# Adding up the token rows during the final expert item, and finishing only that item's 128 slots after it

## What is computed

```python
def moe_swiglu(x, w_router, b_router, w_g, w_u, w_d):
    logits = (x @ w_router).astype(jnp.float32) + b_router.astype(jnp.float32)
    top_v, top_i = lax.top_k(logits, TOP_K)          # TOP_K = 2 of 8 experts
    top_w = jax.nn.softmax(top_v, axis=-1)
    ...
    for e in range(N_EXPERTS):
        y = y + combine[..., e:e + 1] * swiglu(x, w_g[e], w_u[e], w_d[e])
    return y
...
x = layer_norm(ALPHA * x + f, p['ln2_g'][l], p['ln2_b'][l])
```

## Time and profile before

| | us |
|---|---|
| median of 3 runs (1659.34 to 1661.12) | 1660.32 |
| the profiled execution: its time | 1659.13 |
| the profiled execution: its span | 1657.3 |
| last matmul of the last item ends | about 1616.3 |
| from there to the end of the span | 41.0 |

### The profile page before, as it was taken

The page is one execution under the profiler, slowest core; times in us unless marked ns, Lnnn a source line. Parts: engine busy times, 40 slices in busy tenths (PEclk is TensorE's granted clock), DMA queues, the critical chain, the costliest instruction groups (busy, mean ns, idle before and its releaser), DMA issues.

```text
span 1657.3 us, 20014 instructions
## 1 busy us (share of the span) xinstructions
PE 1584.7 (96%) x7315; PEld 1265.9 (76%) x7315; DVE 1155.0 (70%) x1312; ACT 810.4 (49%) x1093; POOL 178.0 (11%) x115
## 2 busy tenths in 40 slices
PE   8999999999999999999999999789999999999990
PEld 7877777888888888888777788467777777777770
DVE  6888747584444423379887584698888888888886
ACT  5344442253223222163444422667777777777771
POOL 0410005151000000005000060200000000000006
PEclk9999999999999999999999999899999999999995
...
DMA packets 134380, 325.69 MB, mean 197 GB/s; under 512 B 7984, under 2 KB 19632, under 8 KB 133808
## 3 DMA queue, kind: packets, MB, share of 16 engines
...
## 4 chain that ended last, share of the span: by engine, by line
PE 94%; DVE 3%; ACT 1%; DMA 1%; issue 1%; POOL 0%; SPq 0%; ACTq 0%; DVEq 0%
PE bank L1312 15%; PE bank L1313 15%; PE bank L1314 15%; PE bank L1593 9%; PE bank L1595 9%; PE bank L1594 9%; PE bank L1352 4%; PE bank L1351 4%; PE bank L1350 4%; PE bank L1601 3%; PE bank L1572 1%; PE bank L1424 1%; PE bank L1437 1%; DVE X L1182 1%; PE bank L1409 1%; PE bank L1305 1%
## 5 line engine op out<-in xcount | busy, mean ns | idle before, releaser
L821 DVE TENSOR_TENSOR wlo<-raw,whi 128x1024 fp32r<-128x1024 f32 x170 | 239.0, 1408 | 207.5 <-ACT whi L522 207.2
L1312 PE MATMUL bank<-xth,whi 128*128 128x512 f32 (+1 forms) x976 | 381.5, 391 | 1.8 <-DVE wlo L821 1.8
L1313 PE MATMUL bank<-xtl,whi 128*128 128x512 f32 (+1 forms) x976 | 370.8, 380 | 0.0
L1314 PE MATMUL bank<-xth,wlo 128*128 128x512 f32 (+1 forms) x976 | 370.5, 380 | 0.0
L1045 DVE TENSOR_TENSOR ewlo<-eraw,ewhi 128x2048 fp32r<-128x2048 f32 x135 | 309.0, 2290 | 66.8 <-ACT ewhi L717 66.7
L717 ACT ACTIVATE ewhi<-eraw 128x2048 fp32r<-128x2048 f32 x135 | 258.0, 1911 | 43.0 <-PE bank L1595 43.0
L522 ACT ACTIVATE whi<-raw 128x1024 fp32r<-128x1024 f32 x170 | 178.6, 1051 | 137.0 <-PE bank L1352 123.9
L1312 PEld LDWEIGHTS bank<-xth,whi 128*128 128x128 f32 x976 | 184.2, 189 | 50.7 <-issue 8.5
L1313 PEld LDWEIGHTS bank<-xtl,whi 128*128 128x128 f32 x976 | 184.2, 189 | 36.4 <-issue 3.8
L1593 PE MATMUL bank<-ewhi,xgh 128*128 128x512 f32 (+1 forms) x528 | 205.9, 390 | 6.0 <-DVE xgl L1112 4.8
L1314 PEld LDWEIGHTS bank<-xth,wlo 128*128 128x128 f32 x976 | 184.1, 189 | 35.3
...
## 6 DMA issues: line engine op xcount, KB each, us to landing
...
raw<-dense_w SPq DMA_DIRECT2D x170, 512.0 KB, 3.4
...
rows<-item_rows ACTq DMA_DIRECT2D x11, 512.0 KB, 7.2
```

Source lines behind the costliest of these rows:

```text
L821: V.tensor_tensor(wlo[:, g % SPL, :], raw[:, g % RAW, :], whi[:, g % SPL, :], ALU.subtract).then_inc(lo_done, 1)
L1312: mm(out, wh, xh, start=first, stop=False)
L1313: mm(out, wh, xl, start=False, stop=False)
L1314: return mm(out, wl, xh, start=False, stop=last)
```

## The change

The final item is taken out of the loop and written out behind it on every engine, without the preparations for a next item. In the routing stage DVE also works out, for each token, whether one of its two rows lies in the final item (`inl`), the weights of the rows that don't (`wrest`, 0 for one that does) and gather indices (`gidx`, row 0 for one that does); a small matmul with a 0/1 matrix `sel_last` gives for each of the final item's 128 slots its token, weight and whether it is used (`mslot`). In the first item eight tiny DVE steps (`last_slots`) turn these into indices.

During the final item POOL gathers the eight tiles of result rows of the items before through three buffers, and DVE adds them to `X` in turn (`add_rest`), one behind each `e_low` from piece step 5 on, and two behind the last. SP stores the four sums to `xd`. ACT takes the mean and variance of tiles 0 to 2 by running sums and normalises them, DVE does tile 3, and DVE applies gain and bias to tiles 0 to 2 (`affine_out`); SP stores all four. These rows are right for every token that has no row in the final item. For the final item's 128 slots POOL gathers the sums back from `xd`, DVE adds the weighted result rows straight from PSUM, normalises them and POOL scatters the 128 rows over the two outputs, each scatter skipping the rows of the other output; it starts when all plain stores have landed. Cut to its core (helpers `e_low`, `hidden_rows` and the rest are as before):

```diff
             for tt in range(TT):
-                if tt < TT - 1:
-                    sp.wait_ge(out_pool, tt + 1)
+                sp.wait_ge(y_added, 2 * tt + 2)
+                sp.dma_start(xd[tt * P:(tt + 1) * P], X[:, tt, :]).then_inc(z_stored, 16)
+            for tt in (3, 0, 1, 2):
+                if tt == 3:
+                    sp.wait_ge(out_pool, 1)
                 else:
-                    sp.wait_ge(y_ready, 1)
+                    sp.wait_ge(y_ready, tt + 1)
                 dst = (y0, y1)[tt // 2]
...
-                if tt < TT - 1:
-                    act.wait_ge(out_norm, tt + 1)
-                    nc.scalar.activation(X[:, tt, :], X[:, tt, :], ACT.Identity, scale=rstd[:, tt:tt + 1],
-                                         bias=nmr[:, tt:tt + 1]).then_inc(ln_norm, 1)
+            for p in range(N_GUP):
+                if p % 2 == 1 or p == 10:
+                    hidden_tanh(p // 2, final)
+                if p % 2 == 0 and 2 <= p < 10:
+                    hidden_high(p // 2 - 1, final)
+                e_split(p + ESPL, final)
+                if p == 2:
+                    act.wait_ge(e_out, final * 16 + 16)
+                    act.wait_ge(rows_tr, final * 2 + 2)
+                    act.wait_ge(xg_lo, final * 2 + 2)
+                    nc.scalar.activation(begun[:, :], eps[:, 0:1], ACT.Copy).then_inc(rows_free, 1)
+            hidden_high(4, final)
+            e_split(14, final)
+            hidden_high(5, final)
+            act.wait_ge(e_lo, final * NSP + ERING)
+            for tt in range(TT - 1):
+                x = X[:, tt, :]
+                act.wait_ge(y_added, 2 * tt + 2)
+                nc.scalar.activation(junk, x, ACT.Copy, accum_out=mom[:, tt, 0:1]).then_inc(sum_done, 1)
+                act.wait_ge(sum_done, 2 * tt + 1)
+                nc.scalar.activation(mom[:, tt, 1:2], mom[:, tt, 0:1], ACT.Copy, scale=-1.0 / D).then_inc(mean_done, 1)
+                act.wait_ge(mean_done, tt + 1)
+                nc.scalar.activation(junk, x, ACT.Square, bias=mom[:, tt, 1:2],
+                                     accum_out=mom[:, tt, 2:3]).then_inc(sum_done, 1)
+                act.wait_ge(sum_done, 2 * tt + 2)
+                nc.scalar.activation(rstd[:, tt:tt + 1], mom[:, tt, 2:3], ACT.Sqrt, bias=eps[:, 0:1],
+                                     scale=1.0 / D).then_inc(out_sd, 1)
+                act.wait_ge(out_rs, tt + 1)
+                act.wait_ge(z_stored, 16 * TT)
+                nc.scalar.activation(x, x, ACT.Identity, scale=rstd[:, tt:tt + 1],
+                                     bias=nmr[:, tt:tt + 1]).then_inc(out_norm, 1)
+                if tt != 1:
+                    i = tt // 2
+                    act.wait_ge(ln_mv, 3 * TT + i + 1)
+                    nc.scalar.activation(rstd[:, TT - 1:TT], mv[:, i, 1:2], ACT.Sqrt,
+                                         bias=eps[:, 0:1]).then_inc(ln_sd, 1)
...
-            V.tensor_tensor(mixk[:, 1, :], etmp[:, 1, :], mixk[:, 0, :], ALU.mult).then_inc(rt_mix, 1)
+            step(V.tensor_tensor(mixk[:, 1, :], etmp[:, 1, :], mixk[:, 0, :], ALU.mult))
+            step(V.tensor_scalar(lastb[:, :], end[:, 7:8], float(CAP), -float(CAP), ALU.mult, ALU.add))
+            step(V.tensor_scalar(dist[:, :, :], rowk[:, :, :], lastb[:, 0:1], None, ALU.subtract))
...
+            V.tensor_tensor(wrest[:, :, :], mixk[:, :, :], wlast[:, :, :], ALU.subtract)
+            V.tensor_tensor(about[:, :, 1], wlast[:, 0, :], wlast[:, 1, :], ALU.add)
+            step(V.tensor_tensor(grow[:, :, :], rowk[:, :, :], grow[:, :, :], ALU.subtract))
+            V.tensor_copy(gidx[:, :, :], grow[:, :, :])
+            dve.wait_ge(sel_mm, 2)
+            for tt in range(TT):
+                ins = V.tensor_scalar(sel_last[:, tt, :], slot_no[:, :], place[:, tt:tt + 1], None, ALU.is_equal)
+            ins.then_inc(rt_last, 1)
...
+            def last_slots():
...
...
+                    last_slots()
...
                 item(j)
-            final = sem("final_step")
-            fin = Step(dve, final)
...
+            gain, bias = lngb[:, 0, :], lngb[:, 1, :]
+            def add_rest(g):
+                tt, k = g // 2, g % 2
+                if k == 1:
+                    dve.wait_ge(y_added, g)
+                dve.wait_ge(gathered[g % 3], 16 * (g // 3 + 1))
+                V.scalar_tensor_tensor(X[:, tt, :], ybuf[g % 3], wrest[:, k, tt:tt + 1], X[:, tt, :], ALU.mult,
+                                       ALU.add).then_inc(y_added, 1)
+            for p in range(N_GUP):
+                if p % 2 == 1 or p == 10:
+                    hidden_rows(p // 2, final)
+                if p % 2 == 0 and 2 <= p < 10:
+                    hidden_low(p // 2 - 1, final)
+                e_low(p + ESPL, final)
+                if p >= 5:
+                    add_rest(p - 5)
+            e_low(14, final)
+            add_rest(6)
+            add_rest(7)
...
+            def spread(i, x):
+                V.bn_stats(stats[:, i, 0, :], x[:, 0:512])
+                fin(V.bn_stats(stats[:, i, 1, :], x[:, 512:1024]))
+                V.bn_aggr(mv[:, i, :], stats[:, i, :, :]).then_inc(ln_mv, 1)
+            def scale_rows(i, x):
+                std = rstd[:, TT - 1:TT]
+                dve.wait_ge(ln_sd, 3 * TT + i + 1)
+                fin(V.reciprocal(std, std))
+                fin(V.scalar_tensor_tensor(x, x, mv[:, i, 0:1], gain, ALU.subtract, ALU.mult))
+                return V.scalar_tensor_tensor(x, x, std, bias, ALU.mult, ALU.add)
+            def turn_std(tt):
+                std = rstd[:, tt:tt + 1]
+                dve.wait_ge(out_sd, tt + 1)
+                fin(V.reciprocal(std, std))
+                V.tensor_tensor(nmr[:, tt:tt + 1], mom[:, tt, 1:2], std, ALU.mult).then_inc(out_rs, 1)
+            def affine_out(tt):
+                dve.wait_ge(out_norm, tt + 1)
+                fin(V.tensor_tensor(X[:, tt, :], X[:, tt, :], gain, ALU.mult))
+                V.tensor_tensor(X[:, tt, :], X[:, tt, :], bias, ALU.add).then_inc(y_ready, 1)
             dve.wait_ge(in_ln3, 16)
-            gain, bias = lngb[:, 0, :], lngb[:, 1, :]
-            for tt in range(TT):
-                x, std = X[:, tt, :], rstd[:, tt:tt + 1]
-                dve.wait_ge(x_base, tt + 1)
-                dve.wait_ge(gathered[tt], 32)
-                for k in range(2):
-                    fin(V.scalar_tensor_tensor(x, yg[:, k, tt, :], mixk[:, k, tt:tt + 1], x, ALU.mult, ALU.add))
-                V.bn_stats(stats[:, tt, 0, :], X[:, tt, 0:512])
-                fin(V.bn_stats(stats[:, tt, 1, :], X[:, tt, 512:1024]))
-                V.bn_aggr(mv[:, tt, :], stats[:, tt, :, :]).then_inc(ln_mv, 1)
-                dve.wait_ge(ln_sd, 3 * TT + tt + 1)
-                fin(V.reciprocal(std, std))
-                if tt < TT - 1:
-                    V.scalar_tensor_tensor(nmr[:, tt:tt + 1], mv[:, tt, 0:1], -1.0, std, ALU.mult,
-                                           ALU.mult).then_inc(out_norm, 1)
-                else:
-                    fin(V.scalar_tensor_tensor(x, x, mv[:, tt, 0:1], gain, ALU.subtract, ALU.mult))
-                    V.scalar_tensor_tensor(x, x, std, bias, ALU.mult, ALU.add).then_inc(y_ready, 1)
+            dve.wait_ge(y_added, 2 * TT)
+            spread(0, X[:, TT - 1, :])
+            turn_std(0)
+            dve.wait_ge(z_stored, 16 * TT)
+            scale_rows(0, X[:, TT - 1, :]).then_inc(out_pool, 1)
+            affine_out(0)
+            turn_std(1)
+            affine_out(1)
+            turn_std(2)
+            zs = ybuf[2]
+            dve.wait_ge(base_in, 16)
+            for h in range(2):
+                dve.wait_ge(e_used, final * NPC + (14 + 3 * h))
+                ins = V.scalar_tensor_tensor(zs[:, 512 * h:512 * h + 512], bank[B_Y[h]][:, :], mslot[:, 1:2],
+                                             zs[:, 512 * h:512 * h + 512], ALU.mult, ALU.add)
+            fin(ins)
+            dve.wait_ge(out_pool, 1)
+            spread(1, zs)
+            affine_out(2)
+            scale_rows(1, zs).then_inc(last_ready, 1)
...
-                    pool.indirect_dma_start(out=yg[:, k, tt, :], out_offset=None, in_=yd,
-                                            in_offset=bass.IndirectOffsetOnAxis(ap=ridx[:, k, tt:tt + 1], axis=0)
-                                            ).then_inc(gathered[tt], 16)
-            pool.wait_ge(in_ln3, 16)
-            for tt in range(TT - 1):
-                pool.wait_ge(ln_norm, 3 * TT + tt + 1)
-                step(G.tensor_tensor(X[:, tt, :], X[:, tt, :], lngb[:, 0, :], ALU.mult))
-                G.tensor_tensor(X[:, tt, :], X[:, tt, :], lngb[:, 1, :], ALU.add).then_inc(out_pool, 1)
+            pool.wait_ge(rows_free, 1)
+            for g in range(2 * TT):
+                if g >= 3:
+                    pool.wait_ge(y_added, g - 2)
+                pool.indirect_dma_start(out=ybuf[g % 3], out_offset=None, in_=yd,
```

(23 more changed lines are left out.)

95 lines of the change are left out of this document (68 added, 27 removed).

## The result

| | before | after |
|---|---|---|
| median of 4 runs each (lowest to highest) | 1660.62 us (1659.34 to 1661.12) | 1646.62 us (1643.94 to 1648.52) |
| the profiled execution: time, span | 1659.13, 1657.3 | 1647.25, 1645.4 |
| last matmul ends | about 1616.3 | about 1620.7 |
| from there to the end | 41.0 | 24.7 |

The ratio after to before is 0.9919, with a 95% interval of 0.9907 to 0.9932: the kernel became faster, by 14.0 us in the medians and 11.9 in the profiled spans. The median before of 1660.32 that the prediction used is that of the first three of these four runs.) The prediction said 1648.5 us (1644 to 1656) and a span of 1645.5.

What follows compares the result with a forecast made beforehand. TensorE was taken as the bound (94% of the chain), outside a 41.0 us tail. Sums ready at 1615.3 plus 30.2 gave span 1645.5, 11.8 shorter; profiled execution 1647.3, plus 1.2 for the median: 1648.5 us, range 1644 to 1656.

Steps and rivals of the forecast that it cites:

- front and routing: Before item 0: about 3.3 us of added VectorE steps fit into idle time, priced at 0, up to 1 us.
- last `e_low` ends: Final item, VectorE: six additions ahead of it delay it by 6.5 us, from 1606.2 to 1612.7.
- t0: End of the final item's additions on VectorE: the time at which the sums are ready, claimed at 1615.3 us.
- gather, issue to landing: Final item: with at most three in flight a gather takes about 8 us, hidden under a latency limit of 10.7.
- t0 to slots added: Tail: result rows added to the 128 slots in two half-wide steps of 0.7 us, done at t0 + 16.6.
- t0 to VectorE's last step: Tail: serial chain between VectorE and ScalarE until the slots are finished, at t0 + 23.4 us.
- from there to the end: Two scatters, the second issued 1.3 us later and landing 4.9 after that, then half a microsecond: t0 + 30.2.
- The clock: Final item: a fall to 1.2 GHz after a TensorE wait, taken as 0, with 1.7 us for t0 as bound.
- rival 4: More overlaps: a row-skipping scatter lands as a plain store, the adds fit gaps; 1643.5 to 1646 us; chance 0.09.
- rival 2: Final item: a late gather holds VectorE, each microsecond beyond 10.7 us latency paid three times; chance 0.11, 0.05 slower.
- Rival 3: Final item: the hiding doesn't happen, the adds cost TensorE what they saved; 1656 to 1662 us; chance 0.05.
- Rival 1: Tail: the new end is dearer, through scatter landing, VectorE-ScalarE chain or front; 1652 to 1656 us; chance 0.18.

Runs made afterwards that it cites:

- the second profile: The changed kernel unedited, run again beside three versions built on it; span 1647.3 us, median 1647.45, ratio to the kernel before 0.9923.
- the run with the sums first: Changed kernel with ScalarE taking the sums of tiles 0 to 2 first and normalising afterwards; span 1644.0 us, median 1646.56, ratio to the kernel before 0.9921.

## Why the prediction was right, point by point

| step of the sum | predicted | measured |
|---|---|---|
| front and routing | 0, up to 1 | 0.0, in the second profile 0.6 |
| last `e_low` ends | 1612.7 | 1612.4 |
| t0 | 1615.3 | 1615.0 |
| TensorE ends | near 1621 | 1620.7 |
| gather, issue to landing | about 8 | 7.0, at most 9.2 |
| t0 to tile 3 finished | 7.2 | 7.4 |
| t0 to tile 1 normalised | 11.4 | 11.3 |
| t0 to slots added | 16.6 | 15.9 |
| t0 to VectorE's last step | 23.4 | 22.5 |
| from there to the end | 6.8 | 7.9 |
| span | 1645.5 | 1645.4 |

**The final item.** The first item of the kernel before was the right place to read: the same step behind the same `e_low` cost 1.28 us, and the waits came to 2.01 and 1.84 instead of about 2. The delay of the last `e_low`, priced at 6.5 us, was 6.2, of which 0.3 arose ahead of the item (an `e_low` of 1577.88 before starts at 1578.19 now).

**Front.** Ahead of routing nothing of the change stands, so its price is read from ScalarE's logits step to the first matmul of item 0: 17.9 us before (1048.68 to 1066.61), 18.0 and 18.6 in the two profiles of the changed kernel. The bound of 1 held.

**The clock** was taken at 0, with 1.7 us for t0 as a bound, because a fall would lie in time that TensorE waits anyway. The two profiles of the changed kernel, one with the fall and one without, show just that for the final item: t0 and TensorE's end keep their distance, and the second wait shrinks from 1.84 to 0.27. What the prediction had not reckoned with is that the falls in the routing stage and in the first item, which cost 1.6 and 0.7 us, come and go from one execution to the next. Its own rows had the fall in the first item, the first profile of the changed kernel did not, so some 0.7 of the 11.9 us between the two profiled spans is luck.

**The chain.** Between t0 and tile 1 each mark is right to 0.2 us. Then one term was too large: ScalarE's sums for a tile take 2.9 us (1.05, 0.19, 0.20, 1.15, 0.19 and 0.29, less overlaps), not 3.4, and since the slots wait behind tile 2's sums, that is 0.6 of the 0.9 us in which the chain was shorter.

**The end** hid errors of opposite sign. The second scatter, which ends the chain, landed 2.7 us after its issue, like a plain store, and not after the gather's 4.9 to which I had held it nearest. One half of rival 4's condition came true, worth 2.2 us; the other, that the additions fit gaps, did not. But from VectorE's last step to the first issue went 0.85 us, where I had none, and from the last landing to the end of the span 3.0, where I had 0.5, the 0.4 of the kernel before. By luck the part was only 1.1 us off. What those 3.0 us consist of no run shows; they are the same in all eight profiles that end with the scatters and 0.4 in the two that end with plain stores. The Trainium skill ("DMA: Bandwidth & Descriptors", "Anatomy of one DMA — SWDGE (gpsimd) path") gives 2.0 us plus the bytes at 436 GB/s. For half of the 0.34 MB that the two scatters moved that is an estimate of 2.4 us, against 3.2 and 2.7 measured, and for the 512 KB of the gather of the 128 sums 3.2 us, against 4.5.

**The gathers.** The row that spoke against the change, a 2.70 us issue beside VectorE, repeats: five of eight issues took 2.5 to 3.1 us, all begun while an `e_low` ran, and three 0.94, begun beside short steps that read one of their inputs from PSUM. This agrees with the Trainium skill, "GPSIMD Engine Reference", "Key points", on steps with two SBUF inputs, only that not every issue was hit; 9.8 us by its rule was nearer to the largest latency (9.2) than to the median. One step of the prediction was wrong here without showing in the time: it took 10.7 us as what every gather may take. The first seven had 10.0 to 12.5 us from issue to use, but the last had 7.1. At the 8 us that the prediction took for each it would have held VectorE by 0.9 us, and rival 2 would have begun at 7.1 us of latency and not at 10.7. It landed in 4.4. The latencies fell from 9.2 to 4.4 us along the item while its weight loads ended (the last landed at 1596.5); that this is the cause is not shown.

**The median** was taken 1.2 us above the profiled execution, as before; after, it lies 0.6 below it. That is nearly all of the 1.9 us between 1648.5 and 1646.62: the profiled execution itself was predicted at 1647.3 and took 1647.25.

**What the rivals were worth.** Rival 3, an item that pays back what it hides, is answered by the tiny additions (the end follows t0, not TensorE) and by the additions put behind (12 us lost). Rival 2 was made to happen by one gather in flight and costs 25.6 us then (1671.0 to 1645.4). Rival 1 is seen in the part from the landing on, at 2.5 us more than I had. One reason that I gave after the prediction, for the run with the sums first, was shown wrong by that run: I took the 1.31 us wait of VectorE for late sums, and it is the normalising pass, which the prediction's own chain had there (+ 10.1 to + 11.4).
